# A hybrid decoder layer on one core: three scratch tiles lent to the gathers of expert rows for more of the program

## The reference, cut to what matters

```python
def block(args):                       # 128 tokens at a time, 8 blocks
    xb, ib, gb = args
    u = jnp.take(u_tab, ib, axis=0)    # 128 tokens x 128 picks x 1024 float32
    coef = gb * jax.nn.gelu(jnp.einsum('cd,ced->ce', xb, u), approximate=False)
    return jnp.einsum('ce,ced->cd', coef, jnp.take(v_tab, ib, axis=0))
```

## Time and profile before

| | |
|---|---|
| time, median of 3 runs | 3568.58 us (3562.12 to 3576.55) |
| the profiled execution | 3574.2 us |
| its span, first to last instruction | 3572.5 us |
| busy: PE, DVE, POOL, ACT | 77%, 66%, 55%, 15% of the span |
| moved by DMA | 1246.47 MB, mean 349 GB/s |
| chain that ended last: PE, DVE, "issue", unknown, DMA | 36%, 19%, 14%, 14%, 10% |

### The profile page before, as it was taken

How to read it: one execution, slowest core, us unless ns; L and a number is a source line. 1 busy time by engine, 2 the same in 40 slices (tenths; PEclk the granted TensorE clock), 3 DMA queues, 4 the chain that set the end, 5 groups by cost and what they waited for, 6 DMA issues and landing times.

```text
span 3572.5 us, 41983 instructions
## 1 busy us (share of the span) xinstructions
PE 2748.3 (77%) x15556; PEld 1282.6 (36%) x15556; DVE 2363.9 (66%) x6051; ACT 518.6 (15%) x1152; POOL 1969.0 (55%) x2093
## 2 busy tenths in 40 slices
PE   9899886888888789986756685667656777667777
PEld 7777762333333323333313332233323331212111
DVE  5678889676676657767677767777677747665200
ACT  3221311110111102011011101010111101111101
POOL 0013345555655556556665666656666666666663
PEclk9999997999999899997867887788767888788899
DMA  6558998899998999989999999999999999999995
GB/s 220 202 185 303 356 352 301 323 362 378 382 355 321 368 372 386 372 321 406 383 364 334 367 410 360 367 336 407 383 359 334 389 407 403 378 375 380 383 348 226
DMA packets 385149, 1246.47 MB, mean 349 GB/s; under 512 B 40496, under 2 KB 75056, under 8 KB 384176
## 3 DMA queue, kind: packets, MB, share of 16 engines
q0 software_dynamic: 294912, 1073.87, 79.2%
q1 hardware_dynamic: 90032, 169.91, 13.3%
HBM read 1216.75 MB, written 26.87 MB: 348 GB/s over the span
## 4 chain that ended last, share of the span: by engine, by line
PE 36%; DVE 19%; issue 14%; another core or an unknown queue 14%; DMA 10%; POOL 5%; ACT 2%; SPq 1%; POOLq 0%; ACTq 0%; DVEq 0%
PE e_acc L1316 9%; DVE e_u L2227 6%; PE e_pl L1404 5%; DMA e_v<-in_v_tab,e_idxT 3%; DMA e_u<-in_u_tab,e_idx 3%; PE e_acc L1361 3%; PE e_pd L1225 3%; PE e_pd L1019 3%; PE e_acc L1386 3%; DVE e_late L2227 2%; PE e_pd L1199 2%; PE e_pd L1124 2%; DVE e_gbc L1950 2%; POOL e_v L992 2%
## 5 line engine op out<-in xcount | busy, mean ns | idle before, releaser
L2227 DVE CUSTOM_DVE_ANT_0 e_u<-e_u,e_c 128x1024 f32<-128x1024 f32 x776 | 941.0, 1213 | 338.6 <-DMA e_u<-in_u_tab,e_idx 251.0
L984 POOL DMA_INDIRECT e_u<-in_u_tab,e_idx x776 | 746.4, 962 | 711.5 <-DVE e_dots L2227 284.8
L1316 PE MATMUL e_acc<-e_v,e_wd 128*32 128x512 f32 x2844 | 828.9, 704 | 197.2 <-DMA e_v<-in_v_tab,e_idxT 141.2
L992 POOL DMA_INDIRECT e_v<-in_v_tab,e_idxT x711 | 676.5, 952 | 487.3 <-PE e_acc L1316 201.1
L1404 PE MATMUL e_pl<-e_late,e_v 128*128 128x512 f32 x608 | 339.6, 656 | 55.1 <-DVE e_side L2040 15.7
L2227 DVE CUSTOM_DVE_ANT_0 e_late<-e_late,e_c 128x1024 f32<-128x1024 f32 x248 | 300.2, 1212 | 106.0 <-DMA e_late<-in_u_tab,e_idx 61.9
L984 POOL DMA_INDIRECT e_late<-in_u_tab,e_idx x248 | 240.2, 968 | 166.5 <-DVE e_dots L2227 111.2
L1316 PE MATMUL e_acc<-e_late,e_wd 128*32 128x512 f32 x832 | 263.5, 698 | 74.8 <-DMA e_late<-in_v_tab,e_idxT 49.7
L1316 PEld LDWEIGHTS e_acc<-e_v,e_wd 128*32 128x32 f32 x2844 | 114.7, 116 | 573.8 <-issue 275.4
L1950 DVE SCALAR_TENSOR_TENSOR e_gbc<-e_hc,e_cw,e_gbc 128x128 f32<-128x128 f32 x960 | 303.5, 343 | 0.4
L992 POOL DMA_INDIRECT e_late<-in_v_tab,e_idxT x208 | 197.1, 947 | 139.0 <-issue 49.0
(11 more groups left out here) (298 smaller groups left out, 3215.2 us busy)
## 6 DMA issues: line engine op xcount, KB each, us to landing
e_u<-in_w_in SPq DMA_DIRECT2D x38, 512.0 KB, 3.7
e_v<-in_w_in SPq DMA_DIRECT2D x38, 512.0 KB
e_v<-in_w_in SPq DMA_DIRECT2D x76, 256.0 KB
e_u<-in_u_tab,e_idx POOLq DMA_INDIRECT x776
e_zb<-in_w_c SPq DMA_DIRECT2D x48, 256.0 KB
e_v<-in_v_tab,e_idxT POOLq DMA_INDIRECT x711
e_arena<-in_w_r SPq DMA_DIRECT2D x32, 256.0 KB
e_zb<-in_w_r SPq DMA_DIRECT2D x32, 256.0 KB
```

Of the source, the lines that this page charges most:

```text
L984: pool.indirect_dma_start(out=rows_in[i], out_offset=None, in_=io["u_tab"], in_offset=bass.IndirectOffsetOnAxis(ap=idx[n % 2][:, j:j + 1], ...
L992: pool.indirect_dma_start(out=rows_in[i], out_offset=None, in_=io["v_tab"], in_offset=bass.IndirectOffsetOnAxis(ap=idxT[n % (LAG + 1)][:, ...
L1316: last = pe.matmul(acc[rows, cols], w[:, at_:at_ + 32], rows_in[row][:, cols], start=(step == 0), stop=True, skip_group_check=True)
L2227: dve.tensor_tensor_reduce(rows_in[i], rows_in[i], c[:, :], 1.0, 0.0, ALU.mult, ALU.add, dots[n % 2][:, j:j + 1]).then_inc(s_dot, 1)
```

## The change

`LENT` is longer. Before, `e_gt` and `e_x` were lent in the second to fourth period; now in the second to seventh: `e_gt` from slot 106 of the period before to slot 54, `e_x` from slot 26 to slot 72. `e_side` is a new lent buffer from g = 448 (slot 64 of the fourth period) to g = 884 (slot 116 of the seventh). The loads of x and of the first half of the gates, which stood in slot 30 for the later blocks, stand in slots 84 and 66 there too (`lent = n >= 2`). Two semaphores became one (`s_w_tail` is counted on `s_w_out`), with the same waits.

```diff
-ROWS = UW + VW + LW + 2
+ROWS = UW + VW + LW + 3
...
-GATE_ROW, X_ROW = ROWS - 2, ROWS - 1
+GATE_ROW, X_ROW, SIDE_ROW = ROWS - 3, ROWS - 2, ROWS - 1
...
-LENT = {GATE_ROW: [(1, SLOTS, SLOTS + GATES_AT - 12), (2, SLOTS + MIX_AT + 40, 2 * SLOTS + GATES_AT - 12),
-                   (3, 2 * SLOTS + MIX_AT + 40, 3 * SLOTS + GATES_AT - 12)],
-        X_ROW: [(1, SLOTS, SLOTS + X_AT - 12), (2, 2 * SLOTS + 26, 2 * SLOTS + X_AT - 12), (3, 3 * SLOTS + 26, MORE_AT)]}
+LENT = {GATE_ROW: [(1, SLOTS, SLOTS + GATES_AT - 12),
+                   *((t, (t - 1) * SLOTS + MIX_AT + 40, t * SLOTS + GATES_AT - 12) for t in range(2, NT - 1))],
+        X_ROW: [(1, SLOTS, SLOTS + X_AT - 12), *((t, t * SLOTS + 26, t * SLOTS + X_AT - 12) for t in range(2, NT - 1))],
+        SIDE_ROW: [(NT - 1, MORE_AT, (NT - 1) * SLOTS - 12)]}
...
-            among = V_FIRST + lent_now(g, "v") if g < MORE_AT else V_LATER if g < NT * SLOTS else V_LATER + U_LATER
+            among = (V_FIRST if g < MORE_AT else V_LATER) + lent_now(g, "v") if g < NT * SLOTS else V_LATER + U_LATER
...
                     if m == 0:
-                        for i in range(2):
-                            sp.wait_ge(s_lst[i], 16 * stores_until(COL_TILES) // 2)
+                        given_back(SIDE_ROW, NT - 1)
...
             def front(n, s):
-                lent = 2 <= n <= 4
+                lent = n >= 2
...
                 if held and held[0] == "lent" and i == GATE_ROW:
                     pool.wait_ge(s_sq, held[1] + 1)
+                elif held and held[0] == "lent" and i == SIDE_ROW:
+                    for e in range(2):
+                        pool.wait_ge(s_lst[e], 16 * stores_until(COL_TILES) // 2)
```

More of the change, by code:

```diff
@@ L183 @@
 LATE_ROWS = list(range(UW + VW, UW + VW + LW))
-GATE_ROW, X_ROW = ROWS - 2, ROWS - 1
+GATE_ROW, X_ROW, SIDE_ROW = ROWS - 3, ROWS - 2, ROWS - 1
 GATES_AT, X_AT = MIX_AT, MIX_AT + 18
-LENT = {GATE_ROW: [(1, SLOTS, SLOTS + GATES_AT - 12), (2, SLOTS + MIX_AT + 40, 2 * SLOTS + GATES_AT - 12),
-                   (3, 2 * SLOTS + MIX_AT + 40, 3 * SLOTS + GATES_AT - 12)],
-        X_ROW: [(1, SLOTS, SLOTS + X_AT - 12), (2, 2 * SLOTS + 26, 2 * SLOTS + X_AT - 12), (3, 3 * SLOTS + 26, MORE_AT)]}
-LENT_TO = {GATE_ROW: "v", X_ROW: "v"}
+LENT = {GATE_ROW: [(1, SLOTS, SLOTS + GATES_AT - 12),
+                   *((t, (t - 1) * SLOTS + MIX_AT + 40, t * SLOTS + GATES_AT - 12) for t in range(2, NT - 1))],
+        X_ROW: [(1, SLOTS, SLOTS + X_AT - 12), *((t, t * SLOTS + 26, t * SLOTS + X_AT - 12) for t in range(2, NT - 1))],
+        SIDE_ROW: [(NT - 1, MORE_AT, (NT - 1) * SLOTS - 12)]}
+LENT_TO = {GATE_ROW: ("v", "v"), X_ROW: ("v", "v"), SIDE_ROW: ("v", "v")}
 def lent_now(g, kind):
-    return [i for i in LENT if LENT_TO[i] == kind and any(first <= g < end for _, first, end in LENT[i])]
+    return [i for i in LENT if LENT_TO[i][g >= MORE_AT] == kind and any(first <= g < end for _, first, end in LENT[i])]
 def gather_rows():
@@ L223, in gather_rows @@
         if g < NT * SLOTS:
-            take(g, U_FIRST + LATE_ROWS if g < PARK_AT else U_FIRST + lent_now(g, "u") if g < MORE_AT else U_LATER, "u", g, u_rows)
+            take(g, U_FIRST + LATE_ROWS if g < PARK_AT else (U_FIRST if g < MORE_AT else U_LATER) + lent_now(g, "u"), "u", g, u_rows)
     return u_rows, v_rows, parked_after, last_use
@@ L500, in trunk @@
         v, late_x = buf("e_v", [P, VW, D]), buf("e_late", [P, LW, D])
-        rows_in = [u[i][:, :] for i in range(UW)] + [v[:, i, :] for i in range(VW)] + [late_x[:, i, :] for i in range(LW)] + [gt[:, :], xin]
+        rows_in = [u[i][:, :] for i in range(UW)] + [v[:, i, :] for i in range(VW)] + [late_x[:, i, :] for i in range(LW)] + [gt[:, :], xin, xt]
         a_rstd = v[:, 0, :]
@@ L559, in trunk @@
         s_const, s_iota = sem("e_constants"), sem("e_iota_then_spread_buffers_made")
-        s_w_q, s_w_tail = [sem(f"e_query_weights_in{i}") for i in range(len(W_Q_PARTS))], sem("e_tail_weights_in")
+        s_w_q = [sem(f"e_query_weights_in{i}") for i in range(len(W_Q_PARTS))]
         s_ident, s_vec, s_up, s_x = sem("e_identity_made"), sem("e_vectors_in"), sem("e_up_weights_in"), [sem(f"e_xT_pair_in{i}") for i in range(KT // 2)]
@@ L586, in trunk @@
         s_hps, s_h, s_hout = sem("e_h_in_psum"), sem("e_h_ready"), sem("e_h_out")
-        s_w_out, s_keys = sem("e_out_weights_in"), sem("e_keys_in")
+        s_w_out, s_keys = sem("e_out_weights_then_tail_weights_in"), sem("e_keys_in")
         s_fv, s_var, s_rstd = sem("e_h_mean_square"), sem("e_h_variance"), sem("e_h_rstd")
@@ L887, in _ @@
                         sp.wait_ge(s_hps, 2 * NT)
-                        sp.dma_start(w_ple[:, :, :], io["w_ple"]).then_inc(s_w_tail, 16)
+                        sp.dma_start(w_ple[:, :, :], io["w_ple"]).then_inc(s_w_out, 16)
                         sp.wait_ge(s_qps, 2 * NT)
-                        sp.dma_start(w_proj, io["w_proj"]).then_inc(s_w_tail, 16)
-                        sp.dma_start(g_fin, io["g_fin"].to_broadcast([P, D])).then_inc(s_w_tail, 16)
+                        sp.dma_start(w_proj, io["w_proj"]).then_inc(s_w_out, 16)
+                        sp.dma_start(g_fin, io["g_fin"].to_broadcast([P, D])).then_inc(s_w_out, 16)
                     if tail_step(t, s):
@@ L1270, in tail_turned @@
                     pe.wait_ge(s_qT, 2 * NT)
-                    pe.wait_ge(s_w_tail, 16 * 3)
+                    pe.wait_ge(s_w_out, 16 * (1 + 3))
                 turned(tail_h(m), s_ttr)
```

## The result

| | before | after |
|---|---|---|
| time, median | 3570.42 us (3562.12 to 3576.55, 4 runs) | 3646.01 us (3638.06 to 3654.65, 4 runs) |
| the profiled execution, its span | 3574.2, 3572.5 us | 3643.67, 3642.0 us |
| fifth, sixth, seventh period (first dots) | 387, 380, 398 us | 408, 412, 409 us |

A forecast was written before the change was run, and what follows sets the result against it. It took DMA bytes to bound the kernel except in the recurrence, paced by a chain of small steps. Terms -10.2 - 3 + 3.9 - 2 + 1.6 = -9.7 us gave 3559 us against the median, range 3528 to 3580 us.

The forecast's parts named there:

- What bounds it now: Bytes bound most stretches, small steps the recurrence (slots 26 to 66); sooner gathers pay only from slot 66 to period's end.
- Term 1, the ends: Slots 106 to 128, fourth to seventh period: nine v buffers keep POOL from stopping; -10.2 us.
- Term 2, the stock: At slot 66: POOL further ahead when the recurrence ends, limited by u buffers; 1 us a period, -3 us.
- Term 3, the loads: x's load moves into the full stretch, +3.9 us; slots 12 to 26 are freed of loads, -2 us.
- Term 4, the waits: New waits on POOL: `e_side` at g = 449 waits once for a late store, +1.6 us; the others cost nothing.
- POOL's waits: From 1620 us on, v waits on PE shrink from 187 us to well under 100; waits for `e_dots` grow.
- slower: Rival, 13%: from slot 66 on, unpaused gathers delay SP's mixer weight loads, pushing back dependent work; 17 us, 3586 us.
- It doesn't reach the time: Rival, 15%: DMA engines have no room at the period ends, v waits become u waits; 3569 to 3574 us.
- The rule against term 1: HBM ceiling of about 358 GB/s per core: period ends already past full, their gain nil, sum near nought.

The follow-up runs named there:

- before_thin: Kernel before, but v gathers fetch 512 of 1024 columns, except the first into a buffer or after its loan; 3575.01 us, 0.9945 of the kernel before.
- moved_loads_again: Kernel before with its own buffers, only the loads of x and the first half of the gates moved to slots 84 and 66; 1.0002 of the kernel before.
- landed_cap: Changed kernel, but each v gather also waits until the u gather of two slots before has landed; 1.1143 of the kernel before.
- after_thin: Changed kernel with v gathers of 512 of 1024 columns, as in before_thin; 3643.87 us, 1.0141 of the kernel before, 1.0197 of before_thin.

## Why the prediction was wrong, point by point

- **What bounds it now.** "What sets the pace is the chain of small steps" was right for the chip that was measured, and before_thin shows it (0.9945 with a quarter of the row bytes gone). The failed step is the next one: "a gather issued sooner pays only between slot 66 and the period's end" took a sooner gather to be free in the recurrence. The stretches were to keep 127 to 130 us; they took 145 to 147, and holding POOL's lead to seven rows by one added wait took back two thirds of the loss with whole rows and 51 of 69 us with thinner ones. In the first pair of traces the slowing shows in a step of the chain (30 to 77 us over six visits). The prediction put a longer lead in the recurrence at nothing, so no term had it, and the range ended at 3580.
- **Term 1, the ends:** -10.2 forecast for slots 106 to 128 of the fourth to seventh period. The fourth, forecast at -5.1, gave -0.8 us; the fifth and sixth, forecast at -1.7 and -3.4, took 6.2 and 13.6 us more, at 382 and 370 GB/s where 400 or more was expected; the seventh took 1.2 less. Room in the DMA was a bound, not a gain. What makes the ends longer isn't shown. Ahead of them slots 84 to 98 took 12 us more and 98 to 106 12 less, which cancels.
- **Term 2, the stock:** -3 forecast, -3.2 us in slots 66 to 84. The agreement may be luck: with the buffers as before, moved_loads_again took 4.9 us more there, so that stretch moves by more than the term.
- **Term 3, the loads:** x's load stands at 2071.67 us, at slot 80, as told. +3.9 - 2 forecast; moved_loads_again measured 1.0002 (within 8 us of nothing), and its three periods came to 1170 us against 1164. In the whole change slots 12 to 26 were 4.4 us longer, not 2 shorter.
- **Term 4, the waits:** right in kind. POOL's gather into `e_side` at 1600.24 us shows [2.47 <-DMA mixer_gates<-e_side], where 1.6 and the usual 0.3 were expected.
- **POOL's waits:** v waits fell less than told (187 to 104, not well under 100), u waits grew, as told. That was read as harmless.
- **The rivals:** "slower" had the sign but not the mechanism. L1127 waited for no load (PE's waits from 2026 to 2110 us name "issue" 7.6 and ACT 4.5 us for it), and `h` (L2116) stood 0.0 us. "It doesn't reach the time" is what the second kind shows (0.9993, with the DMA full throughout). Its reason gave the DMA share at the ends as 0.99 to 1.01; the seventh period's row has 1.02, which only helps it.
- **The rule against term 1:** the ceiling of about 358 GB/s (the Trainium skill, "DMA: Bandwidth & Descriptors", section "Where 436 GB/s comes from") was weighed and set aside. The second kind holds 408 GB/s over a whole recurrence, so setting it aside was right, and it gave no help with the sign.

What stays open is why PE takes instructions slowly, and why on one kind of chip only. The Trainium skill, "Runtime: NRT & Kernel Launch", section "Instruction fetch mechanics", says that each engine's instructions come in blocks of 16 KiB, 256 instructions, and that the cost of a block is mostly hidden. The trace agrees on the size of the blocks, 2.02 MB in 123 packets, and has the same number on both kinds of chip:

```profile
q8 instruction: 123, 2.02, 0.2%
```

In five of the six slow episodes of the changed kernel no packet of this queue moved at all; around the first they stand at 1908.7 and 1938.5 us. So no run here shows that fetching is the cause, and these times speak against it. Also open: which loan carries how much (both runs of each fell on the second kind), whether it is the lead of v rows or the number of gathers in flight that does it; and how the loss comes about where the step is not what grows. In after_thin the step of L1091 explains only 12 of the 57 us that its recurrences lost, and PE's idle time without a wait only 15 (29 to 45 us); PE's waits for ACT grew too (41 to 69 us).

## What to carry to other kernels

More buffers are not free where no consumer waits for rows: here they took 83 us of waits off POOL's v gathers, put 140 us on its u gathers, and on one kind of chip slowed the chain that binds. Before lending a buffer, ask in which stretch a consumer waits for a landing (here from slot 66 on); to lend it there alone was not tried here. And put a price, with both signs, on an edit that lets a producer run ahead through a stretch bound by a chain. A verdict of 2% may belong to one kind of chip: run the kernel before again with every group.

## What the runs showed of the hardware

- Chips differ by 6 to 7% on this kernel (3361 against 3570 to 3595 us), at DMA packets of the same length (4096 bytes in 0.159 and 0.161 us, median), DVE products of the same length (1210 and 1220 ns) and ACT's (473 and 460 ns). The difference is PE's: 128 against 103 us for the same recurrence, at a mean granted clock of 0.76 against 0.90 of 2.4 GHz in it, and idle times without a wait on the slower kind alone.
- PE can take instructions singly or in small groups 0.7 or 1.4 us apart for 12 us, without a wait. It begins at a granted clock of 1.00 (1924 to 1927 us), and PE is quick again at 0.50 (1936 us).
- Four gathers in flight (a v and a u gather of two slots, 512 KB each) kept the DMA at 277 and 283 GB/s (landed_cap), where the kernel before moves 333 to 412 with more in flight.
